# A two-block transformer kernel on one core: the order of work in the retention, in the gated recurrence, and in the last four value chunks

## The reference

```python
# first block
h = rms_norm(x); proj = h @ w_in                    # 1024 -> 2840, in column blocks of 512
q, k = rope(rq), rope(rk)                           # 4 retention heads, 64 wide
o = ((q @ k.T) * decay) @ rv                        # decayed, causal; value heads 128 wide
y_ret = silu(rg) * group_norm(o)                    # mean and variance per token and head
y_nsa = sparse_attention(rope(nq), compressed(kcm, vcm), rope(ksl), vsl, rope(kwn), vwn, gates)
x = x + rms_norm(concat(y_ret, y_nsa) @ w_out)
x = x + rms_norm(conv_ffn(rms_norm(x)))
# second block
mod = silu(c) @ w_ada + b                           # shifts, scales, gates
p = modulated_norm(x) @ w_in_2
f = lb + (1 - lb) * sigmoid(f_raw)                  # gated linear recurrence (4 heads of 128):
state_t = f_t * state_{t-1} + k_t v_t;  o_t = q_t state_t
y_a = group_rmsnorm(o) * silu(g)
y_b = group_rmsnorm(b_gate * conv(c_gate * xin))    # short convolution, 4 groups of 128
x = x + gate1 * (concat(y_a, y_b) @ w_out_2)
x = x + gate2 * peer(modulated_norm(x))             # 16384 experts, dense here: gelu(x @ U.T), weighted, @ V
return rmsnorm(x)
```

## Time and profile before

| | us |
|---|---|
| median of 3 runs | 2809.83 (2808.03 to 2818.89) |
| the profiled execution's own time | 2808.66 |
| its span in the profile | 2806.8 |
| PE busy | 2708.3 (96% of the span) |
| DVE busy, ACT busy | 1512.1, 1078.3 |
| PE waiting for the vector engine's queue at barriers, in all | 19.1 |

### The profile page before, as it was taken

The page is one execution under the profiler, slowest core; times in us unless marked ns, Lnnn a source line. Parts: engine busy times, 40 slices in busy tenths (PEclk is TensorE's granted clock), DMA queues, the critical chain, the costliest instruction groups (busy, mean ns, idle before and its releaser), DMA issues.

```text
span 2806.8 us, 33380 instructions
## 1 busy us (share of the span) xinstructions
PE 2708.3 (96%) x13009; PEld 2246.4 (80%) x13009; DVE 1512.1 (54%) x2480; ACT 1078.3 (38%) x1468; POOL 202.7 (7%) x127
## 2 busy tenths in 40 slices
PE   7989998999999996999999999999999999999997
PEld 6867777888887884788888888888888888888886
DVE  4364654655535664477677565656324444444444
ACT  4344453433325435433333345555433333333332
POOL 0010000000000000000011233333000000000000
PEclk9988999999999997999999999999999999999998
DMA  5223343223332220333444454545565655566552
GB/s 194 85 67 98 113 128 90 87 93 97 100 96 82 83 75 23 113 103 104 152 141 146 126 180 164 215 167 212 194 235 193 206 194 187 184 202 199 187 187 83
DMA packets 148508, 392.11 MB, mean 140 GB/s; under 512 B 10944, under 2 KB 44752, under 8 KB 146832
## 3 DMA queue, kind: packets, MB, share of 16 engines
q1 hardware_dynamic: 94176, 274.86, 30.9%
q10 hardware_dynamic: 51904, 102.77, 10.4%
q0 software_dynamic: 2288, 12.54, 1.2%
HBM read 318.82 MB, written 71.30 MB: 139 GB/s over the span
## 4 chain that ended last, share of the span: by engine, by line
PE 93%; DVE 3%; ACT 2%; issue 1%; DMA 0%; DVEq 0%; POOL 0%; SPq 0%; ACTq 0%; POOLq 0%
PE PS L263 27%; PE PS L264 27%; PE PS L265 27%; PE PS L1940 4%; PE PS L1719 1%; PE PS L1856 1%; PE PS L1803 1%; PE PS L1790 1%; PE PS L407 1%; DVE WL L258 1%; PE PS L1918 1%; DMA RAW<-in_w_in 0%; PE PS L413 0%; PE PS L1722 0%; ACT A L443 0%
## 5 line engine op out<-in xcount | busy, mean ns | idle before, releaser
L258 DVE TENSOR_TENSOR WL<-RAW,WH 128x1024 fp32r<-128x1024 f32 x462 | 593.8, 1287 | 801.2 <-ACT WH L252 754.7
L263 PE MATMUL PS<-HH,WH 128*128 128x512 f32 x1696 | 668.1, 394 | 9.8 <-DVE HL L424 8.2
L252 ACT ACTIVATE WH<-RAW 128x1024 fp32r<-128x1024 f32 x462 | 486.1, 1053 | 460.1 <-PE PS L265 440.4
L264 PE MATMUL PS<-HL,WH 128*128 128x512 f32 x1696 | 660.3, 389 | 0.0
L265 PE MATMUL PS<-HH,WL 128*128 128x512 f32 x1696 | 660.2, 389 | 0.0
L263 PE MATMUL PS<-WH,WGH 128*128 128x512 f32 x1024 | 398.5, 389 | 0.7 <-ACT ROW L1007 0.7
L264 PE MATMUL PS<-WL,WGH 128*128 128x512 f32 x1024 | 398.3, 389 | 0.0
L265 PE MATMUL PS<-WH,WGL 128*128 128x512 f32 x1024 | 398.3, 389 | 0.0
L263 PEld LDWEIGHTS PS<-HH,WH 128*128 128x128 f32 x1696 | 318.6, 188 | 79.9 <-DVE HL L424 11.1
L265 PEld LDWEIGHTS PS<-HH,WL 128*128 128x128 f32 x1696 | 318.3, 188 | 66.6
L264 PEld LDWEIGHTS PS<-HL,WH 128*128 128x128 f32 x1696 | 318.7, 188 | 62.6
(11 more groups left out here) (319 smaller groups left out, 2950.9 us busy)
## 6 DMA issues: line engine op xcount, KB each, us to landing
RAW<-in_peer_u SPq DMA_DIRECT2D x128, 512.0 KB, 3.7
RAW<-in_peer_v SPq DMA_DIRECT2D x128, 512.0 KB, 4.3
gate_matrices<-A ACTq DMA_DIRECT2D x8, 4096.0 KB, 13.1
A<-gate_matrices ACTq DMA_DIRECT2D x32, 1024.0 KB, 7.3
A<-acts ACTq DMA_DIRECT2D x32, 1024.0 KB, 10.6
RAW<-in_w_ada SPq DMA_DIRECT2D x48, 512.0 KB, 3.8
RAW<-in_ffn_up SPq DMA_DIRECT2D x44, 512.0 KB, 3.6
acts<-GATE SPq DMA_DIRECT2D x64, 256.0 KB, 2.8
```

The costliest lines, as they stand in the source:

```text
L252: nc.scalar.activation(WHr[:, slot(c), 0:w], RAW[:, slot(c), 0:w], ACT.Copy).then_inc(sem("high_done"), 1)
L258: nc.vector.tensor_tensor(WLr[:, slot(c), 0:w], RAW[:, slot(c), 0:w], WH[:, slot(c), 0:w], ALU.subtract).then_inc(sem("low_done"), 1)
L263: nc.tensor.matmul(out, L[0], R[0], start=first, stop=False)
L264: nc.tensor.matmul(out, L[0], R[1], start=False, stop=False)
```

## The change

Three stretches are written in another order; the arithmetic of the results stays. **Retention:** the turns of `DUP` and of the first four heads go between the chunks of column block 5, heads are turned in the order `HEADS`, the first head's scores follow block 5, and the attention's 12 heads are turned one by one in bank 3 between the scores and outputs of heads 1 to 3. The small ropes stand behind the decays of heads 0 and 1. ACT copies the outputs to `Y` (`gn_copied`), and statistics and norm go into the attention loop at s = 0 to 4, 8, 10, 12 and 13, with the root at s = 5. **Recurrence:** squares, exponentials, convolution and key products go beside value chunks 24 to 27, the decayed keys are turned behind chunk 26, outputs accumulate in banks 4 to 7 and are normed head by head, the barrier goes, and `wout2` starts with the convolution's half (rows k = 4 to 7 first). **The end:** the last four value chunks are multiplied row tile by row tile, the last row tile in two halves, and SP issues the output.

```diff
 def head_bank(n):
-            return (n + 4) % 8 if n < 8 else 2 + n % 2
+            return n if n < 8 else 3
+        HEADS = [0, 4, 1, 5, 2, 6, 3, 7] + [12, 13, 14, 15, 8, 9, 10, 11] + [16, 17, 18, 19]
+        RT_ORDER = (0, 1, 3, 2)
+        RT_AT = {0: (0, 0), 1: (1, 0), 3: (1, 384), 2: (2, 0)}
-        ROPES = {0: (RQ, 8), 3: (NQ, 8), 4: (KSL, 2), 5: (KWN, 2)}
+        ROPES = {0: (RQ, 8), 3: (NQ, 8)}
...
 # SP
-            looped("wout2", 8, lambda m: dr["w_out2"].rearrange("(k p) n -> k p n", p=P)[m])
+            for m in range(NK):
+                k = (m + 4) % NK
+                load((FIRST["wout2"] + m, 0, 0), dr["w_out2"][k * P:(k + 1) * P, :])
+            for t in range(NT):
+                sp.wait_ge(sem("out_ready"), t + 1 if t < NT - 1 else NT + 1)
+                w = D if t < NT - 1 else 512
+                sp.dma_start(dr["out"][t * P:(t + 1) * P, 0:w], X[:, t, 0:w]).then_inc(sem("out_landed"), 16)
+            sp.dma_start(dr["out"][t * P:(t + 1) * P, 512:D], XN[:, t, 512:D]).then_inc(sem("out_landed"), 16)
...
 # ACT, column block 5 and behind it
+                    if b == 5 and q == 1:
+                        for v in range(2):
+                            act.wait_ge(sem("cmp_turned"), v + 1)
...
+                    if b == 5 and q == 2:
+                        store_heads(range(4))
+            store_heads(range(4, 8))
...
+            store_heads(range(8, 18))
             act.wait_ge(sem("rt_scores"), 4 * RH)
...
+            nc.scalar.preload_act_table(ACT.Exp)
+            for t in range(NT):
+                act.wait_ge(sem("rt_out"), RH + t)
+                nc.scalar.activation(Y[:, t, 0:512], PS[:, 4 + t, :], ACT.Copy).then_inc(sem("gn_copied"), 1)
...
                 if s == 5:
+                    act.wait_ge(sem("gn_var"), 1)
+                    nc.scalar.activation(var, var, ACT.Sqrt).then_inc(sem("gn_root"), 1)
...
 # ACT, value chunks
+                if m == 24:
+                    act.wait_ge(sem("lv_scores"), 4 * len(LEVELS))
+                    nc.scalar.activation(SC8, BB, ACT.Exp).then_inc(sem("bb_exp"), 1)
+                if m == 25:
+                    act.wait_ge(sem("dk_diff"), 1)
+                    nc.scalar.activation(SC9, SC9, ACT.Exp).then_inc(sem("dk_exp"), 1)
+                if m == 26:
+                    nc.scalar.preload_act_table(ACT.Ln)
+                    act.wait_ge(sem("cv_done"), 1)
+                    nc.scalar.activation(CC, CB, ACT.Square).then_inc(sem("hg_squares"), 1)
...
 # DVE, attention loop
+                if s < 4:
+                    group_stats(s)
+                if s == 4:
+                    group_variance()
+                if s in (8, 10, 12, 13):
+                    group_normed((8, 10, 12, 13).index(s))
...
 # DVE, value chunks
+                if m == 22:
+                    convolve(0)
+                    convolve(1)
+                if m == 23:
+                    convolve(2)
+                if m == 26:
+                    dve.wait_ge(sem("dk_exp"), 1)
+                    nc.vector.tensor_tensor(SC9, SC9, HK, ALU.mult).then_inc(sem("kd_ready"), 1)
+                if m == 27:
+                    dve.wait_ge(sem("bb_exp"), 2)
+                    nc.vector.tensor_tensor(SC8, SC8, HQ, ALU.mult).then_inc(sem("qx_ready"), 1)
...
 # PE
+                    if b == 5 and q == 1:
+                        pe.wait_ge(sem("proj_stored"), 5)
+                        for v in range(2):
+                            pe.wait_ge(sem("cmp_dup"), v + 1)
...
+            for h in range(1, RH):
+                pe.wait_ge(sem("head_stored"), 2 * h + 2)
+                rt_score(h, 0)
+                turn_head(4 + 4 * h)
+                rt_score(h, 1)
+                rt_score(h, 3)
+                turn_head(5 + 4 * h)
+                rt_score(h, 2)
+                rt_out(h - 1, (0, 1))
+                turn_head(6 + 4 * h)
+                rt_out(h - 1, (2, 3))
+                turn_head(7 + 4 * h)
+            rt_out(RH - 1, range(NT))
...
+                if m == 26:
+                    pe.wait_ge(sem("kd_ready"), 1)
+                    pe.wait_ge(sem("lv_taken"), 32)
...
+            pe.wait_ge(sem("o_normed"), 4)
...
-            barrier(pe, "states")
...
+            for v in range(P - RING):
...
+            for t in range(NT):
+                for n, h in [(n, h) for n in range(RING) for h in range(2)] if t < NT - 1 else \
+                            [(n, h) for h in range(2) for n in range(RING)]:
+                    v = P - RING + n
+                    if t == 0 and h == 0:
+                        pe.wait_ge(sem("low_done"), c0 + QU + v + 1)
+                        pe.wait_ge(sem("w_low"), v + 1)
```

More of the change, by code:

```diff
@@ L199, in wait @@
                 eng.wait_ge(sem(s), v)
-        PHASE_ENDS = ["attention", "turn", "states"]
+        PHASE_ENDS = ["attention", "turn"]
         def barrier(eng, name):
@@ L978, in _ @@
-            barrier(act, "states")
+                nc.scalar.activation(HV[:, t, :], PS[:, t, :], ACT.Copy).then_inc(sem("v_stored"), 1)
+            for n in range(4):
+                act.wait_ge(sem("hg_sums"), n + 1)
+                nc.scalar.activation(CC[:, n, :], PS[:, 4 + n, :], ACT.Ln, bias=con("eps")).then_inc(sem("hg_logs"), 1)
+            for n in range(2):
+                act.wait_ge(sem("hg_logs"), 2 * n + 2)
+                nc.scalar.activation(CC[:, 2 * n:2 * n + 2, :], CC[:, 2 * n:2 * n + 2, :], ACT.Exp, scale=-0.5)                    .then_inc(sem("hg_rstd"), 1)
@@ new lines, in head_high @@
+            def head_high(h):
+                act.wait_ge(sem("y2_ready"), h + 1)
+                nc.scalar.activation(HHr[:, h, :], SC8[:, h, :], ACT.Copy).then_inc(sem("y2_high"), 1)
+            square_of(0)
+            square_of(1)
+            conv_high(0)
+            square_of(2)
+            log_of(0)
+            conv_high(1)
+            square_of(3)
+            for h in range(1, 4):
+                log_of(h)
+            for h in range(4):
+                act.wait_ge(sem("hg_logs"), 4 + h + 1)
+                nc.scalar.activation(SC9[:, h, :], SC9[:, h, :], ACT.Exp, scale=-0.5).then_inc(sem("hg_rstd"), 1)
@@ L979, in _ @@
+            for h in range(4):
+                head_high(h)
             for k in range(NK - 1):
@@ L1435, in _, with head_low @@
+            def head_low(h):
+                dve.wait_ge(sem("y2_high"), 2 + h + 1)
+                nc.vector.tensor_tensor(HLr[:, h, :], SC8[:, h, :], HH[:, h, :], ALU.subtract).then_inc(sem("y2_low"), 1)
+            for n in range(2):
+                conv_low(n)
+            for h in range(4):
+                head_normed(h)
+            for h in range(4):
+                head_gated(h)
+                if h >= 1:
+                    head_low(h - 1)
+            head_low(3)
             for k in range(NK - 1):
@@ new lines, in _ @@
+            pe.wait_ge(sem("hg_squares"), 1)
+            pe.wait_ge(sem("kd_stored"), 3)
+            for n in range(4):
+                nc.tensor.matmul(PS[:, 4 + n, :], con("mean"), CC[:, n, :], start=True, stop=True).then_inc(sem("hg_sums"), 1)
+            for c in range(3):
+                pe.wait_ge(sem("v_stored"), c + 1)
+                for h in range(4):
+                    hs = slice(h * P, (h + 1) * P)
+                    last = nc.tensor.matmul(PS[:, c, hs], KDT[:, c, hs], HV[:, c, hs], start=True, stop=True)
+                last.then_inc(sem("kv_ready"), 1)
@@ new lines, in sums @@
+            def sums(h):
+                pe.wait_ge(sem("hg_squares"), 1 + h + 1)
+                nc.tensor.matmul(PS[:, h, :], con("mean"), SC9[:, h, :], start=True, stop=True).then_inc(sem("hg_sums"), 1)
+            pe.wait_ge(sem("qx_ready"), 1)
+            for h in range(4):
+                for c in range(1, 4):
+                    pe.wait_ge(sem("state_ready"), c)
+                    cs = slice(c * P, (c + 1) * P)
+                    last = nc.tensor.matmul(PS[:, 4 + h, cs], STATE[:, c - 1, h, :], SC8[:, h, cs], start=False, stop=(c == 3))
+                last.then_inc(sem("o_done"), 1)
+                if h >= 1:
+                    sums(h - 1)
@@ new lines, in _, with mixed_ready @@
+            sums(3)
+            pe.wait_ge(sem("o_normed"), 4)
+            def mixed_ready(k):
+                if k >= 4:
+                    pe.wait_ge(sem("y2_low"), (k - 4) // 2 + 1)
+                else:
+                    pe.wait_ge(sem("y2_low"), 2 + k + 1)
+            for m in range(NK):
+                k = (m + 4) % NK
+                mixed_ready(k)
+                if m < NK - 2:
+                    mm_n1(pe, (FIRST["wout2"] + m, 0, 0), (HHr[:, k, :], HLr[:, k, :]), m == 0, False)
@@ L1905, in _ @@
+            mm_n1_by_rows(pe, (FIRST["wout2"] + NK - 2, 0, 0), [(HHr[:, k, :], HLr[:, k, :]) for k in (2, 3)])
             turn_pe(pe, "pre4", XN)
```

401 lines of the change are left out of this document (196 added, 205 removed).

## The result

The changed kernel took 2777.9 us (median of 4 executions, 2773.0 to 2781.1) beside 2809.7 of the kernel before; the ratio is 0.988, with a 95% interval of 0.986 to 0.990. It is faster by 32 us, where 41.5 were forecast. The interval stands for 28 to 40 us, so the forecast gain lies just above it; the time lies in the forecast range (2753 to 2784). The profiled execution has a time of its own of 2780.96 and a span of 2779.2, so the traces compare 2806.8 with 2779.2: 27.6 us.

What follows compares the result with a forecast made beforehand. PE, busy 96% of the span, bounds the kernel; only its waits and lower clock can be won. Retention −10 (−12 and +2 in the loop), recurrence −25, end −6.5 sum to −41.5: 2808.7 becomes 2767 us, range 2753 to 2784.

Steps and rivals of the forecast that it cites:

- all three near their sums: Main case: retention, recurrence and end near −10, −25 and −6.5 us, kernel at 2757 to 2777 us; chance 0.66.
- first rival: Attention loop gives more back through ACT's wait and PE's lower clock: +10 to +20 us, 2777 to 2787; chance 0.18.
- signs of being wrong: PE waiting for `head_turned`'s stores at every head, clock 0.50 in the retention, or the loop growing over 10 us.
- Retention ahead of the loop, forecast −12: Last multiplication of column block 5 to first compression chunk: 48.4 us shrink to 36.5, 12 saved.
- The loop, forecast +2: Attention loop: moved statistics, norm and gate cost 2 us for a table load and root; bounds 0 to 12.9.
- The argument that DVE has holes of 2 us: Attention loop, against more being given back: an engine busy half the time has 2 us holes for each 2 us piece.
- Recurrence, forecast −25: Last value chunk to `wout2`: `wout2` starts at about 1090.9 instead of 1116.0, 25 us saved; bounds −20 to −27.
- The end, forecast −6.5: Last four value chunks to the span's end: shorter work behind PE, less 2.3 us of new waits; bounds −3 to −9.
- the transfer term: Kernel's end: two half-size output transfers from SP's queue put at 4.9 us, where POOL's queue took 5.2.
- the 12 us behind PE: Kernel's end, a sign expected in the profile: the span ends about 12 us after PE.

Runs made afterwards that it cites:

- ret_only: Kernel before with only the change's retention part (turns, scores, ropes, copies, norm in the attention loop): median 2810.3 us, ratio 0.9988 to the kernel before.
- rec_only: Kernel before with only the change's recurrence part: median 2782.8 us, ratio 0.9897 to the kernel before.
- end_only: Kernel before with only the change's end part (last value chunks by row tile, SP's output): median 2804.3 us, ratio 0.9982 to the kernel before.
- norm_late: Changed kernel with the retention's statistics, variance, root, norm and gate moved from s = 0 to 13 of the attention loop to s = 48 to 61: median 2773.8 us.
- cs_wide: Changed kernel with 8 compressed-score multiplications of 32 columns per step replaced by one of 256 at s = 12, 13, 15, 16 (results wrong): median 2771.8 us.
- idle_ahead: norm_late with ACT's copies of the retention outputs each repeated four more times, so PE idles ahead of the attention loop: median 2784.9 us.
- fill_all: norm_late with extra 512-column multiplications: 3 at s = 8 to 19, 4 at later steps without a chunk, 20 in PE's idle time before `wout2`: median 2764.0 us.
- dense: norm_late with 4 extra 512-column multiplications ahead of each score of s = 8 to 19: median 2771.3 us.

## Why the prediction was right, and where it was not

The range held the time, but not because the sum was right. The median of 2777.9 lies just outside what the prediction called "all three near their sums" (2757 to 2777, chance 0.66) and at the start of its first rival (2777 to 2787, chance 0.18), and the profiled 2781 in the midst of it. Of its own signs of being wrong one came true in that execution: the loop grew by over 10 us. The terms for the retention, the recurrence and the end hold; the one for the loop doesn't, and it was too small in its waits and in the clock.

**Retention ahead of the loop, forecast −12: −11.8.** The first compression chunk stands at 179.96; 180 was forecast. The scores of a head take 2.42 and the clock is 1.00 throughout, so the 4.6 of the earlier trace rows and the wait of 5.4 are gone. PE's waits: 0.8 for POOL (1.9 allowed), 0.6 for the first attention head's store behind the table (0.9), 2.1 for `gn_copied` (2). So the waits are 3.5 and not 4.8, and PE's own work is some 33.0 of the 36.5 us and not 31.7: that the sum came out to 0.2 us is partly luck. The decays beside POOL were taken at no cost, between 0 and 0.5 each: their 16 instructions take 280 to 693 ns now, with POOL busy beside the first four, and took 280 to 692 before.

**The loop, forecast +2: +19.2 in the profile.** This is the step that failed, "Given back in the attention loop ... I take 2, the load and its root". Two things were missed. First, the waits. The load stands ahead of the GELU that PE needs at s = 6, and PE waits 2.7 where it waited for nothing; a norm at s = 8 stands ahead of L1303, and PE waits 2.2 for 0.2. The argument that DVE has holes of 2 us looked at the step's length and not at the chain from PE through DVE back to PE within it. Second and larger, the clock: 14.7 us of PE's time. It was named as a rival, at 10 to 20 us with a chance of 0.18, and it is what the profiled execution shows; over more executions it was less. The mean times give an estimate for it. ret_only should be shorter by the 12.0 us ahead of the loop, less 5.1 of new waits, so by 6.9; it is shorter by 3.8, which leaves 3 us (standard error 1.5) for the clock. The changed kernel should be shorter by 11.8 ahead of the loop and by the 29.6 and 6.1 that rec_only and end_only gave, less 4.5 of waits, so by 43.0; it is shorter by 35.7, which leaves 7 us (standard error 3). Both take what one trace shows ahead of the loop and of the waits for every execution. So the loop's clock costs some 3 to 7 us on average, the loop as a whole 8 to 12 instead of 2, and the profiled execution lies at the dear end. The forecast time of 2767 was missed by 10.9 against the median.

**Why the clock is lower in that loop.** Shown: it isn't the two waits (norm_late), not the short multiplications of the compressed scores alone (cs_wide), not a debt from the retention (idle_ahead). Shown too: 48 wide multiplications added in the light steps cut the loss by 14.2 us on average in one kernel, and by 8.5 and 9.9 in two others; a delay without work, of 10 us, did nothing of the kind. So what PE multiplies there matters, though its records are nearly without a gap either way. Open: which property of the added multiplications does it (their width, their rounded inputs or their number were not tried apart), what lets a long piece begin in one execution and not in the next of the same kernel, and why the changed order seems to lose more than the one before, which has the same 1222 multiplications in its loop.

**Recurrence, forecast −25: −26.6 in the profile, −29 (−35 to −23) alone.** The keys' product was ready 0.7 ahead (0.6 to 0.9 forecast). From the last value chunk's end to `wout2` pass 23.7 us, where about 25 were expected, and ACT's chain is what PE waits for at the end (1.7 and 5.5). The slow start stayed: 8.9 us at 0.69, before 0.65.

**The end, forecast −6.5: −8.3 in the profile, −5.1 (−9.3 to −0.8) alone.** PE waits 1.8 and 0.4 for the weights' low parts (1.6 and 0.6 forecast):

```profile
2751.95 0.47 PE L263 MATMUL PS<-WH,WGH 128*128 128x512 f32 x1 [1.83 <-DVE WGL L1661]
2753.94 0.47 PE L263 MATMUL PS<-WH,WGH 128*128 128x512 f32 x1 [0.37 <-DVE WGL L1661]
...
2775.28 0.75 DVE L1717 SCALAR_TENSOR_TENSOR X<-X,MISC,ROW 128x512 f32<-128x512 f32 x1
...
2776.44 0.43 SPq L715 DMA_DIRECT2D out<-A  x1
```

From PE's end at 2771.9 to the last product's end at 2776.0 are 4.1 (4.6 forecast), and from there to the span's end 3.2, where 4.9 were allowed: the transfer term was 1.7 too dear. The two forecast terms make 9.5; the 12 us behind PE that the prediction names among its signs don't follow from them, and 7.3 were measured.

In sum the profiled execution gives −11.8 + 19.2 − 26.6 − 8.3 = −27.5; the forecast's −12 + 2 − 25 − 6.5 = −41.5 misses it by 17.2 in the loop and 0.2 ahead of it, less the 3.4 that recurrence and end gave on top.

## What to carry to other kernels

When work is moved from an idle stretch into a busy loop, follow each moved instruction to what the busy engine needs next on the same queue; holes in an engine's time by themselves say nothing. Where rows show PE busy at the lower clock, treat its time there as a term of its own with its spread over several executions, and look at several executions of each kernel before a few us are credited to an edit: here ret_only alone spread over 12.6 us for a gain of 3.8. Span times clock helps to see where a difference comes from, but it moved by 7 us in one unchanged kernel. Wide multiplications put into light steps paid for themselves in three kernels here (−3.5, +2.1 and −0.9 us for some 10 us of work) and clearly gained only together with those in PE's waits (fill_all); they must be tried over several executions.

## What was not expected of the hardware

- By the rows PE ran 41 us without a gap at a granted clock of 0.53 (norm_late), and with 48 more 128x512 multiplications in the same steps at 0.98 (dense). Being busy by the records doesn't keep the clock up.
- Twenty multiplications in PE's waits of 7.2 us (1.7 and 5.5) took the start of the next stage from 0.69 to 1.00, for 0.1 us (23.8 beside 23.7 from the last value chunk to `wout2`).
- Executions of one unchanged kernel differ by up to 14.5 us (2808.0 to 2822.5 for the kernel before, 57 executions), and the mean clock, 0.981 to 0.974, goes with it.
